# Gated linear attention core: exponent differences, side products and hats on VectorE in joined operations, GpSimd left with the small modulation vectors

## The reference, cut to what matters

```python
def step(s, inp):
    qi, ki, vi, gi = inp
    cum = jnp.cumsum(gi, axis=2)
    diff = cum[:, :, :, None, :] - cum[:, :, None, :, :]
    decay = jnp.exp(jnp.where(mask, diff, -jnp.inf))
    attn = jnp.einsum('bhid,bhjd,bhijd->bhij', qi, ki, decay)
    o = jnp.einsum('bhij,bhjv->bhiv', attn, vi) + jnp.einsum('bhid,bhdv->bhiv', qi * jnp.exp(cum), s)
    last = cum[:, :, -1:, :]
    s_new = s * jnp.exp(last[:, :, 0, :, None]) + jnp.einsum('bhjd,bhjv->bhdv', ki * jnp.exp(last - cum), vi)
    return s_new, o
```

## Time and profile before

| what | us |
|---|---|
| median of 3 runs | 2632.84 |
| lowest, highest | 2632.26, 2637.37 |
| span of the profiled execution | 2625.4 |
| PE busy | 2461.8 (94%) |
| DVE busy | 1358.5 (52%) |
| ACT busy | 1204.7 (46%) |
| POOL busy | 619.5 (24%) |

### The profile page before, as it was taken

How to read it: one execution, slowest core, us unless ns; L and a number is a source line. 1 busy time by engine, 2 the same in 40 slices (tenths; PEclk the granted TensorE clock), 3 DMA queues, 4 the chain that set the end, 5 groups by cost and what they waited for, 6 DMA issues and landing times. The chain is left out here.

```text
span 2625.4 us, 35284 instructions
## 1 busy us (share of the span) xinstructions
PE 2461.8 (94%) x13822; PEld 1970.2 (75%) x13822; DVE 1358.5 (52%) x2133; ACT 1204.7 (46%) x2062; POOL 619.5 (24%) x376
## 2 busy tenths in 40 slices
PE   5997889999998998989999999999999999989989
PEld 3784457788888887668999767577767877768778
DVE  3206667433444767337776534552566355454675
ACT  1833334422326534445654345664357233566364
POOL 1436620000004534210001442002401115503310
PEclk8998989999999999999999999999999999999999
DMA  7235862333333433564665231222321323324335
GB/s 233 81 89 206 281 192 73 112 96 97 96 89 97 129 89 89 192 209 125 176 194 157 73 95 47 60 65 70 81 65 46 106 75 93 113 76 120 82 94 145
DMA packets 417229, 302.15 MB, mean 115 GB/s; under 512 B 10338, under 2 KB 389320, under 8 KB 417064
## 3 DMA queue, kind: packets, MB, share of 16 engines
q1 hardware_dynamic: 415952, 299.45, 38.7%
q10 hardware_dynamic: 1112, 0.44, 0.1%
HBM read 298.80 MB, written 1.05 MB: 114 GB/s over the span
## 5 line engine op out<-in xcount | busy, mean ns | idle before, releaser
L208 POOL TENSOR_TENSOR weights_lo<-wslots,weights_hi 128x1024 fp32r<-128x1024 f32 x158 | 388.2, 2466 | 857.7 <-ACT weights_hi L198 857.1
L198 ACT ACTIVATE weights_hi<-wslots 128x1024 fp32r<-128x1024 f32 x398 | 418.6, 1055 | 261.8 <-PE psum L261 215.7
L261 PE MATMUL psum<-input_hi,weights_hi 128*128 128x512 f32 (+1 forms) x1400 | 501.5, 358 | 4.4 <-PEq L855 1.8
L261 PE MATMUL psum<-input_hi,weights_lo 128*128 128x512 f32 (+1 forms) x1400 | 488.8, 349 | 0.0
L261 PE MATMUL psum<-input_lo,weights_hi 128*128 128x512 f32 (+1 forms) x1400 | 488.3, 349 | 0.0
L208 DVE TENSOR_TENSOR weights_lo<-wslots,weights_hi 128x1024 fp32r<-128x1024 f32 x240 | 296.7, 1244 | 182.4 <-ACT weights_hi L198 181.7
L261 PEld LDWEIGHTS psum<-input_hi,weights_hi 128*128 128x128 f32 x1400 | 264.7, 189 | 44.6 <-issue 7.5
L261 PEld LDWEIGHTS psum<-input_lo,weights_hi 128*128 128x128 f32 x1400 | 265.0, 189 | 38.8 <-issue 3.1
L261 PEld LDWEIGHTS psum<-input_hi,weights_lo 128*128 128x128 f32 x1400 | 264.5, 189 | 38.2
L261 PE MATMUL psum<-ffn_hidden_hi,weights_hi 128*128 128x512 f32 (+1 forms) x512 | 172.0, 336 | 0.0
L261 PE MATMUL psum<-ffn_hidden_hi,weights_lo 128*128 128x512 f32 (+1 forms) x512 | 171.7, 335 | 0.0
(11 more groups left out here) (471 smaller groups left out, 4905.2 us busy)
## 6 DMA issues: line engine op xcount, KB each, us to landing
wslots<-w_in SPq DMA_DIRECT2D x132, 512.0 KB, 4.0
wslots<-ffn_w SPq DMA_DIRECT2D x128, 512.0 KB, 4.0
wslots<-ada_w SPq DMA_DIRECT2D x96, 512.0 KB, 4.9
wslots<-ssd_w_in SPq DMA_DIRECT2D x49, 512.0 KB, 3.9
wslots<-w_ada SPq DMA_DIRECT2D x48, 512.0 KB, 4.5
wslots<-gla_w_in SPq DMA_DIRECT2D x25, 512.0 KB, 3.8
wslots<-w_br SPq DMA_DIRECT2D x24, 512.0 KB, 3.6
wslots<-ssd_w_out SPq DMA_DIRECT2D x16, 512.0 KB, 4.8
```

What stands on the lines that cost most here:

```text
L198: act.activation(self.part(self.whi_r, n), self.slot(n), ACT.Copy)\
L208: engine.tensor_tensor(self.part(self.wlo_r, n), self.slot(n), self.part(self.whi, n), ALU.subtract)\
L261: ins = pe.matmul(out_of(self.bank(g)), l, r, start=first and i == 0, stop=last and i == len(pairs) - 1, skip_group_check=not (first and l ...
```

## The change

All seven levels' operations on both sides move to VectorE. The forward and the backward difference are two operations of 512 elements (`make_diffs`); `ak` and `bq` become the two halves of one tile `sides`, which lies as `qk` does, so that one operation of 1024 elements multiplies both. The hat differences move to VectorE as they are, and the hats become two operations of 1024 elements, one for keys and one for queries. TensorE and ScalarE wait for one semaphore where they waited for two; their work is the same. GpSimd's list holds only the vectors.

```diff
-        ak = b.sb(st, "gla_ak", [P, 2, T])
-        bq = b.sb(st, "gla_bq", [P, 2, T])
+        sides = b.sb(st, "gla_sides", [P, 2, 2, T])
+        bq, ak = sides[:, :, 0, :], sides[:, :, 1, :]
...
-        def make_diff(engine, z, q):
+        def make_diffs(dve, q):
             h, s = q // NL, SIZES[q % NL]
             if q >= 2:
-                engine.wait_ge(b.sem("factors_ready"), b.nth("factors_ready", q - 1))
-            x = cum[:, z, h, :].rearrange("p (n i) -> p n i", i=2 * s)
-            edge = x[:, :, s - 1 + z:s + z].broadcast_to([P, T // (2 * s), 2 * s])
-            engine.tensor_tensor(diff[:, z, q % 2, :].rearrange("p (n i) -> p n i", i=2 * s), x, edge, ALU.subtract)\
-                .then_inc(b.tick(f"diff_ready_{z}"), 1)
+                dve.wait_ge(b.sem("factors_ready"), b.nth("factors_ready", q - 1))
+            for z in range(2):
+                x = cum[:, z, h, :].rearrange("p (n i) -> p n i", i=2 * s)
+                edge = x[:, :, s - 1 + z:s + z].broadcast_to([P, T // (2 * s), 2 * s])
+                ins = dve.tensor_tensor(diff[:, z, q % 2, :].rearrange("p (n i) -> p n i", i=2 * s), x, edge, ALU.subtract)
+            ins.then_inc(b.tick("diffs_ready"), 1)
...
-                make_diff(pool, 1, 0)
...
+                for r in range(4):
+                    finish_vectors(r)
                 finish_vectors(4)
...
+                def hat_diffs(h):
+                    if h:
+                        dve.wait_ge(b.sem("hat_factors"), b.nth("hat_factors", 2 * h))
                     for z in range(2):
-                        dve.wait_ge(b.sem("hat_factors"), b.nth("hat_factors", 2 * h + z + 1))
-                        dve.tensor_tensor(khT[:, z, :], khT[:, z, :], kT[:, h, :], ALU.mult).then_inc(b.tick("key_hat"), 1)
+                        x = cum[:, z, h, :].rearrange("p (c r) -> p c r", r=P)
+                        e = (P - 1) * (1 - z)
+                        dve.tensor_tensor(hd[:, z, :].rearrange("p (c r) -> p c r", r=P), x,
+                                          x[:, :, e:e + 1].broadcast_to([P, CH, P]), ALU.subtract)\
+                            .then_inc(b.tick("hat_diff"), 1)
+
+                def hats(h):
+                    dve.wait_ge(b.sem("hat_factors"), b.nth("hat_factors", 2 * h + 2))
+                    dve.tensor_tensor(khT[:], khT[:], kT[:, h:h + 1, :].broadcast_to([P, 2, T]), ALU.mult)\
+                        .then_inc(b.tick("key_hats"), 1)
+                    x = qhT[:, h % 2]
+                    dve.tensor_tensor(x, x, qT[:, h:h + 1, :].broadcast_to([P, 2, T]), ALU.mult).then_inc(b.tick("query_hats"), 1)
...
-                make_diff(dve, 0, 0)
+                make_diffs(dve, 0)
                 for h in range(GH):
                     for n in range(NL):
                         q = h * NL + n
                         if q + 1 < Q:
-                            make_diff(dve, 0, q + 1)
+                            make_diffs(dve, q + 1)
+                        dve.wait_ge(b.sem("factors_ready"), b.nth("factors_ready", q + 1))
+                        x = sides[:, q % 2]
+                        dve.tensor_tensor(x, x, qk[:, h], ALU.mult).then_inc(b.tick("sides_ready"), 1)
+                        if n == 1:
+                            hat_diffs(h)
                         if n == 3:
-                            key_hats(h)
-                        dve.wait_ge(b.sem("factors_ready"), b.nth("factors_ready", q + 1))
-                        x = ak[:, q % 2, :]
-                        dve.tensor_tensor(x, x, kT[:, h, :], ALU.mult).then_inc(b.tick("key_side"), 1)
+                            hats(h)
```

More of the change, by code:

```diff
@@ L1153, in gla_layer @@
         gla_project(b, qT, kT, v, gate, cum)
-        gla_core(b, qT, kT, v, cum, oT, stat)
+        gla_core(b, qk, v, cum, oT, stat)
         gla_out(b, oT, gate, stat)
@@ L1293, in _, with gla_core @@
                     ins.then_inc(b.tick("gate_summed"), 1)
-def gla_core(b, qT, kT, v, cum, oT, stat):
+def gla_core(b, qk, v, cum, oT, stat):
     d = b.dram
+    qT, kT = qk[:, :, 0, :], qk[:, :, 1, :]
     INV = 1.0 / GATE_NORM
@@ L1329, in gla_core @@
         VECTORS_OUT = {(1, 1): 0, (2, 1): 1, (3, 1): 2, (3, 3): 3}
-        FINISH = {(1, 2): 0, (2, 2): 1, (3, 2): 2, (3, 4): 3}
         def pairs(x, s):
@@ L1360, in scores @@
                     if it:
-                        pe.wait_ge(b.sem("key_side"), b.nth("key_side", q + 1))
-                        pe.wait_ge(b.sem("query_side"), b.nth("query_side", q + 1))
+                        pe.wait_ge(b.sem("sides_ready"), b.nth("sides_ready", q + 1))
                     for t in range(TT):
@@ L1371, in turn_keys @@
                     u = 2 * h + z
-                    pe.wait_ge(b.sem("key_hat"), b.nth("key_hat", u + 1))
+                    pe.wait_ge(b.sem("key_hats"), b.nth("key_hats", h + 1))
                     if u:
@@ L1394, in outputs @@
                     pe.wait_ge(b.sem("state_ready"), b.nth("state_ready", 2 * (h + 1) * (CH - 1)))
-                    pe.wait_ge(b.sem("query_hat"), b.nth("query_hat", 2 * (h + 1)))
+                    pe.wait_ge(b.sem("query_hats"), b.nth("query_hats", h + 1))
                     if h:
@@ L1448, in factors @@
                     s = SIZES[q % NL]
-                    for z in range(2):
-                        act.wait_ge(b.sem(f"diff_ready_{z}"), b.nth(f"diff_ready_{z}", q + 1))
+                    act.wait_ge(b.sem("diffs_ready"), b.nth("diffs_ready", q + 1))
                     if q >= 2:
@@ L1581, in take_score @@
                     ins.then_inc(b.tick("score_taken"), 1)
-                def key_hats(h):
+                def hat_diffs(h):
+                    if h:
+                        dve.wait_ge(b.sem("hat_factors"), b.nth("hat_factors", 2 * h))
                     for z in range(2):
-                        dve.wait_ge(b.sem("hat_factors"), b.nth("hat_factors", 2 * h + z + 1))
-                        dve.tensor_tensor(khT[:, z, :], khT[:, z, :], kT[:, h, :], ALU.mult).then_inc(b.tick("key_hat"), 1)
+                        x = cum[:, z, h, :].rearrange("p (c r) -> p c r", r=P)
[9 more added lines that the diff above has]
+                    dve.tensor_tensor(x, x, qT[:, h:h + 1, :].broadcast_to([P, 2, T]), ALU.mult).then_inc(b.tick("query_hats"), 1)
                 def states(h, i):
```

## The result

The changed kernel takes 2641.73 us (median of 5 runs, 2635.05 to 2650.49) beside 2633.62 us for the kernel before. The ratio is 1.0035, with a 95% interval of 1.0019 to 1.0051: slower by 0.35%, some 9 us. The forecast was 2635.4 us, slower by 0.1%, with a range of 2628 to 2641. The direction was right; the size, 2.6 us, was less than a third of the measured one, and the time lies just above the range.

The account below looks back on a forecast made before the run. No engine is full; the prediction took a chain of step, load, step behind S3 as the bound. Heads 1 to 3 at +5.4 and head 0 at -2.8 gave +2.6 us on 2632.84: 2635.4 us, range 2628 to 2641.

Parts of the forecast that it names:

- S3: TensorE's score that needs the product of level 2; forecast 1.76, 1.67 and 2.46 us later in heads 1 to 3.
- chain of loads: Behind the outputs, a slot is reloaded only once its last reader releases it; next-but-one step about 5 us later.
- the step behind the outputs: TensorE's step after the outputs that follow S3; in head 1 it ends 6.60 us after S3 starts, used unchanged.
- heads 1 to 3: Sum of the later S4 in these heads: +1.66 + 1.24 + 2.46 = +5.4 us; ends +3 and +7.5.
- head 2's credit: In head 2, S4 no longer waits 0.47 us for its product, so it is later by only 1.24 us.
- Head 0: Shorter masks and denser vector work bring S4 2.76 us earlier: -2.8 us; ends -0.9 and -5.
- slow: Head 0 gives nothing back as the half clock lasts past n = 4; 2638.2, up to 2641 us; chance 0.25.
- fast: Contention was the price, so shorter VectorE operations spare heads 1 to 3; 2629 or 2626 us; chance 0.15.
- Absorbed: Loads catch up during the late S3; heads 1 to 3 cost nothing net, head 0's gain is lost; 2632.8 us; chance 0.15.

Follow-up runs that it names:

- r3_hat_early: Changed kernel with the hat differences of heads 1 to 3 taken earlier, at level 5 of the head before; ratio 0.9998 to the kernel before.
- r5_late: Kernel before, GpSimd's share kept, with three unread VectorE products of 512 elements at level 1 of heads 1 to 3; ratio 1.0063 to the kernel before.
- r2_filled: Changed kernel with 8 more matmuls filling TensorE's idle time ahead of S3 in heads 1 to 3; ratio 1.0009 to the kernel before.
- r6_head0: Kernel before with all vector work of head 0 on VectorE, not joined, GpSimd beginning with head 1; ratio 0.9981 to the kernel before.
- r1_again: Changed kernel run again without an edit, as a control; median 2645.36 us, ratio 1.0043 to the kernel before.

## Why the prediction was right or wrong

**The place and the chain were right.** The prediction put everything on when S3 starts, and on a chain of loads that does not catch up. S3 was forecast at T + 8.70 (T is the taking of S0) and came at T + 8.95; VectorE's list is a sum of durations and nothing else. Most of the missing 0.25 is in the three pairs of differences, which take 1.20, 1.26 and 1.20 to the next start (288.24 to 289.44, 290.58 to 291.84, 293.24 to 294.44 above), where I had 1.15 for each. From S0 to S3 the heads lost 2.00, 1.92 and 2.71 us, 6.6 together, where the prediction had 5.9. r3_hat_early and r5_late show from both sides that this passes through to the head's end. The next-but-one step starts 5.03 us behind the step after the outputs (261.33 to 266.36), as the chain of loads wants it. One reading was too strong: for head 1's 0.29 and for the 0.47 ahead of head 2's S4 the rows name no releaser (`<-issue`), so that these two waited for vector work was assumed.

**The step that failed is the one from S3 to the step behind the outputs.** The prediction took "263.62 + 1.07 - 258.09 = 6.60" of head 1 and used it unchanged after an idle time of nearly 3 us. That stretch is TensorE's own work, and its duration hangs on the granted clock. I had looked at the clock in head 0, where the earlier trace rows show 0.50 after sparse work, and had not asked whether the wait that the change adds would bring the same to heads 1 to 3. In heads 1 and 2 of the first profile the stretch to the start of that step was 1.63 and 1.51 us longer than before, in head 3 unchanged. To the step's end, as the prediction counted, it took 8.22 us in head 1 (254.17 to 262.39) and 8.10 in head 2, not 6.60. With TensorE kept at work in the same place (r2_filled) this part of the head is back at 5.56 us, so it was the clock. The Trainium skill's page "TensorE: Matmul & The Clock Gate", section "HAM oscillation — how this bites in real kernels", describes waits that return TensorE to the lower clock again and again; the stretches of r5_late agree, 0.66, 0.57 and 0.57 in three heads of three. It should have been a rival with a price.

For heads 1 to 3 the prediction forecast 5.4 us, and 10.1 were measured (3.9, 3.6 and 2.6). Of the 4.7 between, the clock is 3.1, the later S3 is 0.7, and about half of the rest is head 2's credit (below). The whole span grew by 7.8 us: head 0 gave back 0.9 more than forecast, and stages outside the core added 1.4 that have no cause here. The median lies a little further above its span than before (8.5 us, not 7.4). So the failed step explains the miss in the core; the rest of the median's miss is not explained.

**Head 2's credit was wrong in its logic.** I took 0.47 us off because S4 no longer waits for its product. The chain to the head's end runs over the load that the step ahead of S4 has released, so S4's wait lay beside it. From that step to the next S0 the head took 24.38 before (301.46 to 325.84) and 24.55 after (302.83 to 327.38): nothing came back.

**Head 0 was right, with room.** Forecast -2.8, measured -3.7. The masks, on VectorE's timeline of head 0:

```profile
208.38 0.23 DVE L1538 TENSOR_SCALAR gla_masks<-half_ones 128x128 uint8<-128x128 f32 x1 [1.09 <-DMA gla_diag<-c_diag]
208.52 0.95 DVE L1540 TENSOR_TENSOR gla_masks<-gla_state 128x768 uint8<-128x768 f32 x1
```

They take 1.1 us against 3.09 in the earlier trace rows, where 1.3 were forecast, and would have started another 1.09 earlier but for the load of the diagonal, which I had not looked at. S4 starts 17.2 us behind S0 instead of 20.1, 2.9 earlier, where 2.8 were forecast. The rest is the clock, back at 1.00 sooner: S4 takes 1.16 us instead of 2.04, and over the 20 us that begin some 17 us behind S0 the granted clock is 0.99, where it was 0.80 before (222.3 to 242.3). The stretches 210 to 220 and 220 to 240 of the changed kernel:

```profile
210.00:220.00 10.00, 5.22 (x24) 3.77 (x24) 10.00 (x15) 5.75 (x17) 0.00 (x0) 0.51 0.27 111
220.00:240.00 20.00, 15.99 (x91) 6.13 (x88) 14.45 (x20) 6.03 (x17) 0.00 (x0) 0.99 0.83 284
```

This also answers the "slow" rival. Its sign was a first step of n = 4 no earlier than 234.9; that step starts at 228.37, 25.0 us behind S0 instead of 29.2. Head 0 did bring its gain, so a time beyond that rival's came by another way. The "fast" rival's ground was real, as r6_head0 shows, but it is the order of VectorE's list that decides whether heads 1 to 3 see any of it. "Absorbed" is refuted by r3_hat_early and r5_late.

**The range** reached 2641 for a VectorE that costs a little more an operation. It had no term for the lower clock in heads 1 to 3, and so was too narrow on the side where that term lies.

## What to carry to other kernels

Freeing an engine from contention is worth what its order lets through: work that stands between a late input and the operation that others wait for is on the path, even on an engine that is half idle. When an edit adds an idle time to TensorE, price the work behind it at the lower clock as well, at least as a rival, and look whether the other engine's list can do its independent work before it waits. Here that reordering alone was worth about twice what the move cost. Without the move it still gained 0.15%, with a core as short as that with the move.

## What the runs showed of the hardware that I had not expected

- With waits of 2.8 to 2.9 us ahead of S3 TensorE met the lower clock in four heads of six (changed kernel and r1_again), with waits of 3.7 to 4.05 in three of three, and with waits of 1.61 in none of three. The four are heads 1 and 2 of both profiles, and the two that kept the clock are both head 3. Whether chance or something about head 3's place decides is open. The same wait at another place of the same program can thus cost 1.5 to 1.6 us or nothing. Waits for loads are no clearer: behind one of 2.36 us the clock fell (r1_again, 368.46), behind one of 2.56 it did not (r1_again, 233.16).
- TensorE work that yields nothing made a kernel faster: 8 added matmuls in each of three heads took it from 1.0043 to 1.0009.
- A conversion of 128 elements took 1.29 us while GpSimd was making its product (209.45 to 211.22 of the kernel before), 0.23 in the changed kernel and 0.22 in r6_head0, both without GpSimd. I had read its row as work, not as waiting for its turn.
